# SSD decay weights in a hybrid attention and Mamba-2 trunk kernel: the step's logarithm moves into the exponent as ScalarE's bias, and VectorE's mask and C·B product become one operation each

## The reference

```python
cum = jnp.cumsum(dtc * a, axis=1)                        # per head, a negative
seg = cum[:, :, None] - cum[:, None, :]                  # (t, s)
decay = jnp.exp(jnp.where(causal, seg, -jnp.inf))
cb = jnp.einsum('btgn,bsgn->btsg', cc, bc)               # C . B, the same for all heads of a group
w = cb[..., None] * decay * dtc[:, None]                 # the decay weights
y = jnp.einsum('btsgh,bsghp->btghp', w, xc)
y = y + jnp.einsum('btgn,bghpn->btghp', cc, s) * jnp.exp(cum)[..., None]
s = jnp.exp(cum[:, -1])[..., None, None] * s + ...       # the state carried to the next chunk
```

## Time and profile before

| | |
|---|---|
| median of three executions | 3172.23 us (3167.62 to 3173.3) |
| the profiled execution | 3165.16 us, its span 3163.4 us |
| TensorE matmul busy | 2982.6 us, 94% |
| TensorE weight load busy | 2735.8 us, 86% |
| VectorE busy | 1414.1 us, 45% |
| ScalarE busy | 739.7 us, 23% |
| GpSimd busy | 772.5 us, 24% |

### The profile page before, as it was taken

One profiled execution on the slowest core, in us unless ns is written; L12 is line 12 of the kernel. 1 busy time (PEld: TensorE's weight loads), 2 busy tenths in 40 slices (PEclk: granted clock), 3 DMA queues, 4 the chain that ended last, 5 costly groups with the idle time before them and its releaser, 6 DMA issues.

```text
span 3163.4 us, 46615 instructions
## 1 busy us (share of the span) xinstructions
PE 2982.6 (94%) x17791; PEld 2735.8 (86%) x17791; DVE 1414.1 (45%) x2828; ACT 739.7 (23%) x1680; POOL 772.5 (24%) x535
## 2 busy tenths in 40 slices
PE   7989999999999999999999997999979999999997
PEld 6978997898889888998989994447979999999997
DVE  5584567546764766122232323326673222222235
ACT  4322133213312331222222322211330000000003
POOL 3222222322222222312121210012222223222232
PEclk9999999999999999999999998999989999999999
DMA  5524343333333342221221316773201111111111
GB/s 172 172 92 149 95 129 91 123 116 117 117 96 129 109 145 68 84 57 48 64 67 50 81 43 195 251 233 129 71 27 52 41 47 42 47 47 41 48 51 61
DMA packets 328076, 300.28 MB, mean 95 GB/s; under 512 B 25520, under 2 KB 295392, under 8 KB 326280
## 3 DMA queue, kind: packets, MB, share of 16 engines
q1 hardware_dynamic: 243576, 240.95, 24.7%
q10 hardware_dynamic: 84296, 56.40, 6.0%
HBM read 248.66 MB, written 102.39 MB: 111 GB/s over the span
## 4 chain that ended last, share of the span: by engine, by line
PE 87%; DVE 7%; issue 2%; DMA 2%; ACT 1%; POOL 0%; ACTq 0%; DVEq 0%; SPq 0%; POOLq 0%
PE ps L1979 23%; PE ps L1980 22%; PE ps L1981 22%; DVE ssde L1504 3%; PE ps L2124 2%; PE ps L2360 2%; PE ps L2238 2%; PE ps L2259 2%; PE ps L2306 1%; PE ps L2131 1%; PE ps L2130 1%; PE ps L2176 1%; PE ps L2173 1%; PE ps L2250 1%; DVE rs L1602 1%
## 5 line engine op out<-in xcount | busy, mean ns | idle before, releaser
L1979 PE MATMUL ps<-hH,wH 128*128 128x368 f32 (+1 forms) x2208 | 744.8, 337 | 6.1 <-issue 3.9
L1980 PE MATMUL ps<-hL,wH 128*128 128x368 f32 (+1 forms) x2208 | 726.3, 329 | 0.0
L1981 PE MATMUL ps<-hH,wL 128*128 128x368 f32 (+1 forms) x2208 | 726.2, 329 | 0.0
L723 POOL CAST wH<-wraw 128x1024 fp32r<-128x1024 f32 (+1 forms) x181 | 190.4, 1052 | 1646.6 <-PE ps L1981 1297.5
L1979 PEld LDWEIGHTS ps<-hH,wH 128*128 128x128 f32 x2208 | 418.7, 190 | 46.4 <-issue 40.4
L725 POOL TENSOR_TENSOR wL<-wraw,wH 128x1024 fp32r<-128x1024 f32 (+1 forms) x181 | 438.3, 2421 | 14.5
L1980 PEld LDWEIGHTS ps<-hL,wH 128*128 128x128 f32 x2208 | 418.8, 190 | 0.0
L1981 PEld LDWEIGHTS ps<-hH,wL 128*128 128x128 f32 x2208 | 418.2, 189 | 0.0
L1979 PE MATMUL ps<-mH,wH 128*128 128x368 f32 (+1 forms) x1128 | 372.0, 330 | 12.7 <-DVE mL L1853 7.7
L1980 PE MATMUL ps<-mL,wH 128*128 128x368 f32 (+1 forms) x1128 | 370.5, 328 | 0.0
L1981 PE MATMUL ps<-mH,wL 128*128 128x368 f32 (+1 forms) x1128 | 370.3, 328 | 0.0
(11 more groups left out here) (360 smaller groups left out, 4613.1 us busy)
## 6 DMA issues: line engine op xcount, KB each, us to landing
wraw<-in_w_in_dram SPq DMA_DIRECT2D x92, 512.0 KB, 3.8
wraw<-in_w_up_dram SPq DMA_DIRECT2D x44, 512.0 KB, 3.8
ssdcr<-cum_scr ACTq DMA_DIRECT2D x32, 512.0 KB, 4.9
out_dram<-in_cache_kv_w_dram SPq DMA_DIRECT2D x16, 960.0 KB, 5.5
smkraw<-in_cache_kv_w_dram SPq DMA_DIRECT2D x45, 256.0 KB, 6.8
wraw<-in_w_down_dram SPq DMA_DIRECT2D x22, 512.0 KB, 3.6
smkraw<-in_cache_kv_w_dram SPq DMA_DIRECT2D x9, 1024.0 KB, 5.9
smvraw<-in_cache_kv_w_dram SPq DMA_DIRECT2D x35, 256.0 KB
```

The source lines that it names most:

```text
L723: pool.tensor_copy(hi, a).then_inc(w_hi, 1)
L1979: pe.matmul(dst, hi, cols(mH[:, k, :], c), start=k == 0, stop=False)
L1980: pe.matmul(dst, hi, cols(mL[:, k, :], c), start=False, stop=False)
L1981: last = pe.matmul(dst, lo, cols(mH[:, k, :], c), start=False, stop=k == kt - 1)
```

## The change

The token's factor dt moves into the exponent: exp(x)·dt = exp(x + ln dt). Table slot 0 now holds ln(max(dt, 1.1e-19)) - cum in place of cum, so that:

- `seg(c)` is one VectorE operation for all eight heads: cumrow plus the mask.
- `decay(c)` is eight ScalarE Exp, one for each head, each with slot 0 of its head as a bias that is read per partition.
- `weigh(c)` is one VectorE operation for all heads: times C·B.
- In the chain ahead of the loop VectorE has one operation more (the max), ScalarE one Ln more, and one copy becomes a subtraction.

```diff
@@ ACT, ahead of the loop
             act.activation(dl[:, :, :], du[:, :, :], ACT.Ln).then_inc(dt_act, 1)
-
-            act.wait_ge(dt_dve, 13)
+            act.wait_ge(dt_dve, 12)
+            act.activation(dr[:, :, :], dr[:, :, :], ACT.Ln).then_inc(dt_act, 1)
+
+            act.wait_ge(dt_dve, 14)
@@ ACT, decay(c)
-                    act.activation(dec[c % 2][0:n, :, 0:n], dec[c % 2][0:n, :, 0:n], ACT.Exp).then_inc(exp_done, 1)
+                    for h in range(HG):
+                        ins = act.activation(dec[c % 2][0:n, h, 0:n], dec[c % 2][0:n, h, 0:n], ACT.Exp, bias=tokg[0:n, c, 0, h:h + 1], scale=1.0)
+                    ins.then_inc(exp_done, 1)
@@ DVE, ahead of the loop
+            step(dve.tensor_scalar(dr[:, :, :], dv[:, :, :], 1.1e-19, None, ALU.max))
@@
-            step(dve.tensor_copy(tokd[:, :, :, 0, :].rearrange("p g t e -> p t g e"), cumt[:, :, :].rearrange("p t (g e) -> p t g e", g=SG)))
+            dve.wait_ge(dt_act, 8)
+            step(dve.tensor_tensor(tokd[:, :, :, 0, :].rearrange("p g t e -> p t g e"), dr[:, :, :].rearrange("p t (g e) -> p t g e", g=SG),
+                                   cumt[:, :, :].rearrange("p t (g e) -> p t g e", g=SG), ALU.subtract))
@@ DVE, seg(c)
-                    for h in range(HG):
-                        ins = dve.scalar_tensor_tensor(out=dec[c % 2][0:n, h, 0:n], in0=cumrow[c % 2][0:n, h, 0:n],
-                                                       scalar=tokg[0:n, c, 0, h:h + 1], in1=mask[0:n, 0:n],
-                                                       op0=ALU.subtract, op1=ALU.add)
-                    ins.then_inc(seg_done, 1)
+                    dve.tensor_tensor(dec[c % 2][0:n, :, 0:n], cumrow[c % 2][0:n, :, 0:n],
+                                      mask[0:n, 0:n].unsqueeze(1).to_broadcast([n, HG, n]), ALU.add).then_inc(seg_done, 1)
@@ DVE, weigh(c)
-                    for h in range(HG):
-                        ins = dve.scalar_tensor_tensor(out=dec[c % 2][0:n, h, 0:n], in0=dec[c % 2][0:n, h, 0:n],
-                                                       scalar=tokg[0:n, c, 1, h:h + 1], in1=bcb[0:n, P:P + n],
-                                                       op0=ALU.mult, op1=ALU.mult)
-                    ins.then_inc(w_done, 1)
+                    dve.tensor_tensor(dec[c % 2][0:n, :, 0:n], dec[c % 2][0:n, :, 0:n],
+                                      bcb[0:n, P:P + n].unsqueeze(1).to_broadcast([n, HG, n]), ALU.mult).then_inc(w_done, 1)
```

More of the change, by code:

```diff
@@ L951, in _ @@
             act.activation(dl[:, :, :], du[:, :, :], ACT.Ln).then_inc(dt_act, 1)
-            act.wait_ge(dt_dve, 13)
+            act.wait_ge(dt_dve, 12)
+            act.activation(dr[:, :, :], dr[:, :, :], ACT.Ln).then_inc(dt_act, 1)
+            act.wait_ge(dt_dve, 14)
             act.activation(tokd[:, :, :, 3, :].rearrange("p g t e -> p t g e"), cumt[:, :, :].rearrange("p t (g e) -> p t g e", g=SG),
                            ACT.Exp).then_inc(dt_act, 1)
-            act.wait_ge(dt_dve, 14)
+            act.wait_ge(dt_dve, 15)
             act.activation(de[:, :, :], de[:, :, :], ACT.Exp).then_inc(dt_act, 1)
             act.wait_ge(dt_ps, 6)
-            act.wait_ge(dt_dve, 16)
+            act.wait_ge(dt_dve, 17)
             act.activation(cexp[:, 0:DB], crow[:, SEQ + DS - 1:T:DS], ACT.Exp).then_inc(dt_act, 1)
             act.dma_start(cum_scr, crow[:, :]).then_inc(dt_scr, 16)
-            act.wait_ge(dt_act, 10)
+            act.wait_ge(dt_act, 11)
             act.dma_start(cl_scr, cexp).then_inc(dt_scr, 16)
-            act.wait_ge(dt_dve, 17)
+            act.wait_ge(dt_dve, 18)
             act.dma_start(tok_scr, tokd[:, :, :, :, :].rearrange("p a b c d -> p a (b c d)")).then_inc(dt_scr, 16)
@@ L1450, in _ @@
             step(dve.tensor_copy(crow[:, SEQ:T], A[4][0:SH, 0:NS]))
-            dve.wait_ge(dt_act, 9)
+            dve.wait_ge(dt_act, 10)
             step(dve.tensor_tensor(tokd[:, :, :, 2, :].rearrange("p g t e -> p t g e"), de[:, :, :].rearrange("p t (g e) -> p t g e", g=SG),
@@ L2069, in chain_rows @@
             def chain_rows():
-                pe.wait_ge(dt_dve, 13)
+                pe.wait_ge(dt_dve, 14)
                 for t in range(NT + 1):
```

## The result

In the first comparison the changed kernel took 3109.16 to 3123.15 us against a median of 3167.91 before, a ratio of 0.9836 (0.9817 to 0.9855). One of its executions took 7387.54 us, with the matmuls of 368 columns at twice their time (683 ns in the largest group, 341 in the kernel before; why is not known), and is left out of this; as it was the one with the profile, the profile of the same kernel from a later measurement (`e1_after`) is used here. There it took 3112.99 us, median of 5, against 3169.07, a ratio of 0.9822 (0.9806 to 0.9839): 56 us less, or 52 by the first comparison. The forecast was 3113, 59 less. The profiled execution is 3116.89 us long, its span 3114.9.

What follows compares the result with a forecast made beforehand. TensorE was taken as the bound, holding 87% of the chain, with VectorE counting only where TensorE waits for `weigh`. Terms: 64.1 - 4.0 - 1.2 = 58.9 us less, from the median 3172.2 to 3113 us; range 3103 to 3139.

Steps and rivals of the forecast that it cites:

- What hung on `weigh`: Late `weigh` at chunks 2, 5 and 8 costs 64.1 us: 55.8 in four scans, 8.3 behind chunk 8.
- the three ends: Long `weigh` in chunks 2 and 5: at once, behind the CAST, or behind the subtraction; first two taken, no TensorE wait.
- The rival with the subtraction in front: Chunks 2 and 5: long operation enters behind GpSimd's subtraction; 2.3 us waits and dips stay, 33.4 us lost, 3147; chance 0.08.
- weigh(8): At chunk 8, the halved product is done at 529.3, ahead of TensorE at 530.7; the whole 4.71 us wait goes.
- cm and bm: Behind `scan(8)`, TensorE waits about 1.0 us a group for VectorE; cost 4.0 us in four groups, 2.0 to 5.6.
- The clock behind chunk 8: From the states' transposes to the first product, the low clock goes, giving back about 8.3 us in four groups.
- a rival that had 0.15: Short wait for `bm` amid small matmuls keeps the dip behind chunk 8: 8.3 us less gain, 3122 us; chance 0.15.
- decay(0): Ahead of the scan, eight Exp delay ScalarE; TensorE waits at the fourth z third, 1.2 us in four groups, 0 to 4.
- seg, off the path: Merging `seg` on VectorE saves about 1 us a chunk, but off the path.
- The chain ahead of the loop: One more VectorE operation and one ScalarE Ln before the loop cost nothing, or under 0.5 us once if the table load is late.
- The sum: Whole kernel: 64.1 - 4.0 - 1.2 = 58.9 us less than before, so 3113 us on the median.

Runs made afterwards that it cites:

- e1_after: The changed kernel, unaltered, measured once more for a profile: 3112.99 us, ratio 0.9822 against the kernel before.
- e3: Changed kernel, but `weigh` stays eight operations with dt, slot 0 holding -cum; `seg` one operation, Exp eight: 3170.35 us, ratio 1.0009 against the kernel before.
- e4: Kernel before plus three lines: GpSimd starts weight splits behind chunks 2, 5 and 8 only when VectorE has finished that chunk's weights: 3108.94 us, ratio 0.9812.
- e7: Changed kernel, but in chunks 2 and 5 VectorE starts the one long product only when GpSimd's split is complete: 3154.7 us, ratio 0.9946 against before.
- e2: Changed kernel, but `seg` stays eight operations and the Exp one, slot 0 holding cum - ln dt; only `weigh` is merged: 3122.07 us, ratio 0.9852 against before.
- e5: Changed kernel plus three lines: GpSimd starts splits behind chunks 2, 5 and 8 only when VectorE has finished that chunk's weights: 3100.0 us, ratio 0.9776 against before.
- e6: Changed kernel plus one line: GpSimd starts the two splits behind chunk 8 only when `cm` and `bm` are ready: 3099.3 us, ratio 0.9775 against before.

## Why the prediction was right, step by step

**What hung on `weigh` (64.1 us).** Right in the mechanism: e3 (`weigh` left, nothing gained) and e4 (GpSimd made to wait, 60 us gained without the rewriting) show it from both sides. For the scans I had 55.8; measured, they fell from 335.5 us in all four to 277.5, by 58.0. The 2.2 more come from undisturbed chunks, which take 8.52 to 8.78 us in place of the 8.76 that I took for all.

**When the long operation gets in.** The first of the three ends came, at once, in chunks 2 and 5: 1.31 us, about the 1.2 taken. The prediction called this a narrow race, 0.17 us ahead of the CAST; the outcome was the same in all eight places. The lead alone does not decide it, since `weigh(8)` is recorded 0.21 us ahead of the CAST (509.88, 510.09) and is let in behind it, in all four groups. The rival with the subtraction in front did not come by itself; forced in e7, it costs 33.4 us in the scans, the prediction's own figure, though its split differs (20.9 and 12.5 for 18.4 and 15.0), and 42 in the medians.

**weigh(8)** was let in behind one CAST, as worked out: done 1.79 us after its start, ahead of TensorE (1.7 worked out).

**cm and bm (4.0 us, 2.0 to 5.6).** This term was too small. The wait is 2.05 us a group, 8.2 in all, above my upper bound. The order of events on VectorE was the one named (`bm` behind the subtraction, the copy behind the second CAST), and its time too: the copy is done 3.0 us after `scan(8)` starts (515.93 - 512.93), I had 3.3 at most. What failed is TensorE's side: I took 1.9 us for `scan(8)` from a row that ran wholly at the lower level, as this window of before shows (clock 0.50):

```profile
535.42:537.29 1.87, 1.87 (x16) 1.75 (x17) 1.87 (x5) 1.33 (x2) 0.00 (x0) 0.50 0.14 35
```

At 1.00 TensorE asks for the transposes after 3.22 - 2.08 = 1.1 us. With the long wait gone it is there earlier than the row of before says.

**The clock behind chunk 8 (8.3 us back).** Given back in part only. This small wait in its turn brings the dip in three of four groups of the profiled execution (10.39, 10.63, 10.68 and 9.08 us, against 9.02): 4.7 us in all stay lost. That was the half of a rival that had 0.15. How many groups it strikes differs between executions: behind the same wait of 2.1 us it is two of four in e2's profile and four of four in e7's. From the last `scan` to the first product the four groups took 51.7 us before and take 53.6 now, where the forecast had 47. e5 and e6 show both pieces to be this wait: without it the dip is gone and 13 to 14 us are gained.

**decay(0) (1.2 us, 0 to 4).** The Exp are 0.388 us long and eight of them 2.45, as taken (0.395, 2.5). TensorE's waits for ScalarE at the fourth z third sum to 1.6 us in 3 places, about 4.1 us ahead of `scan(0)`. The place and the size are right, and so is the cause: such waits stand in every profile with eight Exp and in none with one (before, e2, e4). The upper bound was too low: over the other profiles with eight Exp the waits sum to 1.7 to 4.9 us, and single ones reach 2.6 where I had 1.0 at most. What makes them differ so is open.

**seg, off the path.** Wrong as a statement about the changed kernel's parts, though not in the sum, as the change merges both: e2 shows 9 us that hang on it. In the kernel before, the eight short `seg` operations hide behind the late `weigh`; once it is early, they are next in line for GpSimd's split.

**The chain ahead of the loop.** No new wait. The first scan starts 4.0 us later than in the profile before (155.13 for 151.10). But over the seven profiles that have the longer chain it starts between 149.6 and 155.1, and in the two without it at 151.1 and 153.2 (e4). So the 4.0 us are scatter between executions, and a cost of the chain, if there is one, is too small to be seen in it.

**The sum.** Scans -58.0, behind them +1.8, z +1.6: -54.6, beside -52 and -56 measured (58.9 forecast). So the gain was forecast 3 to 7 us larger than measured. Against the sum of the traces it was 2.2 too little in the scans, 6.1 too much behind them, 0.4 too much at the z thirds. That 3113 stands beside a measured 3112.99 is chance: those runs have a median of before 3 us below the one that the forecast started from. The profiled execution alone shows -48.5; of the 6.1 that it is longer than the sum, 4.0 lie ahead of the first scan, and the rest is not traced.

## What to carry to other kernels

When eight short operations take 2.2 us in one place and 5.2 in another, lay the other engine's timeline beside them before counting operations: here GpSimd's split shut VectorE out, three lines of waiting on GpSimd were worth as much as the rewriting (60 and 56 us), and the rewriting with one well placed line was better than either (69). When a long wait goes, read the next operations of the same queue (`add_skip`, `bm`) at TensorE's new, earlier time, at full clock. A short wait in the midst of small matmuls can cost more in the clock behind it: here 8.2 us of waits and 4.7 of clock.

## What the runs showed of the hardware that was not expected

- VectorE and GpSimd hold each other off in both directions: the CAST, 1.10 us in the kernel before, takes 2.04 behind the one `weigh` of 1.31. The Trainium skill (SBUF — State Buffer, "SBUF: two separate sides") says that whoever starts first keeps the shared ports for the whole instruction; the traces agree with it. But they are not let in by strict turns: before, GpSimd's CAST got in behind the first of eight short operations, while in e4 the CAST that came in the midst of the eight of `seg` (455.24, they run to 457.02) took 2.67, so it stood until they were through. What decides between the two is open, and so is why `weigh` is let in ahead of the CAST at chunks 2 and 5 and behind it at chunk 8.
- The small copy (128x64, 0.17 us when alone, as in e6) took 1.02 us beside a CAST: this operation with one SBUF input is held as well.
- The lower clock behind a wait of 2.3 to 2.6 us cost 0.1, 1.8 or 3.4 us in the same program (e7: 8.8, 10.5 and 12.2 us for a chunk that takes 8.71). The kernel before has the same spread behind its waits of 2.6 to 2.8 us: 8.8 us once, 10.5 five times, 11.9 and 12.2. What decides this is open. A wait of 0.4 us at the transposes (e4) was followed by no dip in any group. TensorE's waits of up to 2.2 us for `gpart` stand in every trace; in the one stretch with them that was looked at (the kernel before, 606 to 636 us) the clock stays at 1.00.
